# HGRN scores of a token with itself and with its pair's other token: column sums of products in place of matrix products

## What is computed

```
q, f_f, f_b, v, g = split(h @ w_in)          # 16 heads of 128 features
q = silu(q)
f = lb + (1 - lb) * sigmoid(f_raw);  k = 1 - f        # once for each direction
S_t = diag(f_t) S_{t-1} + k_t v_t^T,   o_t = S_t^T q_t   # forwards and backwards, summed
```

## Time and profile before

| | us |
|---|---|
| median of 3 runs | 2587.51 (2587.24 to 2588.46) |
| the profiled execution, whole | 2589.72 |
| its span, first to last instruction | 2587.9 |
| TensorE matmuls busy in it | 2551.4 |
| VectorE busy | 1684.3 |
| ScalarE busy | 1231.3 |

### The profile page before, as it was taken

One profiled execution on the slowest core, in us unless ns is written; L12 is line 12 of the kernel. 1 busy time (PEld: TensorE's weight loads), 2 busy tenths in 40 slices (PEclk: granted clock), 3 DMA queues, 4 the chain that ended last, 5 costly groups with the idle time before them and its releaser, 6 DMA issues. The chain is left out here.

```text
span 2587.9 us, 32843 instructions
## 1 busy us (share of the span) xinstructions
PE 2551.4 (99%) x13382; PEld 2169.6 (84%) x13382; DVE 1684.3 (65%) x1807; ACT 1231.3 (48%) x1446; POOL 27.8 (1%) x25
## 2 busy tenths in 40 slices
PE   7999999999999999999999999999999999999997
PEld 6878888888888888888888888888788888888886
DVE  6645766555555555555777778785676777777776
ACT  7545344443443444444445454544555444444443
POOL 0000000000000000000000000000000000000000
PEclk9999999999999999999999999999999999999999
DMA  9535445556555555555545454545465555655553
GB/s 358 170 132 163 161 151 177 187 183 194 191 189 191 187 192 189 187 190 176 171 150 175 140 182 134 178 164 180 140 210 188 186 187 188 193 188 187 185 190 114
DMA packets 127413, 465.63 MB, mean 180 GB/s; under 512 B 14208, under 2 KB 14464, under 8 KB 126368
## 3 DMA queue, kind: packets, MB, share of 16 engines
q1 hardware_dynamic: 127264, 463.54, 54.8%
HBM read 461.38 MB, written 2.10 MB: 179 GB/s over the span
## 5 line engine op out<-in xcount | busy, mean ns | idle before, releaser
L1246 DVE TENSOR_TENSOR w_low<-raw,w_high 128x1024 fp32r<-128x1024 f32 x856 | 1042.3, 1224 | 729.2 <-ACT w_high L973 727.1
L973 ACT ACTIVATE w_high<-raw 128x1024 fp32r<-128x1024 f32 x856 | 904.4, 1058 | 922.0 <-PE job L714 507.3
L717 PE MATMUL job<-actA,w_high 128*128 128x512 f32 x3328 | 1180.7, 399 | 1.1 <-DVE actA L1306 1.1
L720 PE MATMUL job<-actA,w_low 128*128 128x256 f32 x3328 | 934.7, 281 | 0.0
L717 PEld LDWEIGHTS job<-actA,w_high 128*128 128x128 f32 x3328 | 626.3, 188 | 156.1 <-DVE actA L1306 1.4
L720 PEld LDWEIGHTS job<-actA,w_low 128*128 128x128 f32 x3328 | 629.5, 189 | 0.7
L712 PE MATMUL job<-w_high,actB 128*128 128x512 f32 x1184 | 463.3, 391 | 10.1 <-DVE w_low L1246 9.9
L713 PE MATMUL job<-w_low,actB 128*128 128x512 f32 x1184 | 461.7, 390 | 0.0
L714 PE MATMUL job<-w_high,actB 128*128 128x512 f32 x1184 | 461.6, 390 | 0.0
L712 PEld LDWEIGHTS job<-w_high,actB 128*128 128x128 f32 x1184 | 222.8, 188 | 57.0 <-issue 9.9
L714 PEld LDWEIGHTS job<-w_high,actB 128*128 128x128 f32 x1184 | 222.8, 188 | 46.9
(11 more groups left out here) (193 smaller groups left out, 1232.0 us busy)
## 6 DMA issues: line engine op xcount, KB each, us to landing
raw<-in_weights SPq DMA_DIRECT2D x856, 512.0 KB, 3.4
M<-in_mem_t SPq DMA_DIRECT2D x4, 512.0 KB, 7.3
slots<-in_mem SPq DMA_DIRECT2D x2, 1024.0 KB, 14.3
M<-in_x_t SPq DMA_DIRECT2D x4, 512.0 KB, 13.8
H<-in_x SPq DMA_DIRECT2D x1, 2048.0 KB, 15.1
out<-H SPq DMA_DIRECT2D x4, 512.0 KB, 2.9
slots<-in_w_small SPq DMA_DIRECT2D x1, 1024.0 KB, 14.1
slots<-in_post_mix_g SPq DMA_DIRECT2D x1, 1024.0 KB, 4.7
```

The lines of the kernel that those rows point to most:

```text
L717: nc.tensor.matmul(J[job.buf][:, x, :], w_high[:, slot, cols], act_both[job.act][:, c, :, :].rearrange("p a t -> p (a t)"), start=begins, ...
L720: mm = nc.tensor.matmul(J[job.buf][:, x, T:2 * T], w_low[:, slot, cols], act_high[job.act][:, c, :], start=False, stop=ends, skip_group_ch ...
L973: nc.scalar.activation(w_high[:, s % AHEAD, :], raw[:, s % RAW_SLOTS, :], ACT.Copy)\
L1246: nc.vector.tensor_tensor(w_low[:, s % AHEAD, :], raw[:, s % RAW_SLOTS, :], w_high[:, s % AHEAD, :].bitcast(F32), ALU.subtract).then_inc(l ...
```

## The change

The two scores that need no matrix product are formed as column sums. For the score of a token with itself VectorE multiplies kk and q elementwise (`sum_product`, "self"); for the other token of the pair it multiplies the queries by the copied keys, read in pairs in reversed order ("pair"). The sum over the 128 features, which lie on partitions, is a product with a 128 x 128 matrix of ones: every row of the result holds all column sums, and the diagonal copy and the mask of level 0 pick from it as before. To be multiplied in the kind of operands that the windows use, each product is split by ScalarE (high) and VectorE (low) into chunks 12 to 15 of the B activations, which are free in these steps (`sum_split`). `column_sums` is then 4 matmuls of 512 columns: high and low for each half of the heads. It takes the place of 8 matmuls in `hgrn_diagonal` and of 8 in `hgrn_level` 0; the matrix of ones becomes an `F32R` tile, written by ScalarE at the start in place of GpSimd. Levels 1 to 6 are as before.

In the plan sum_product(self) comes late in step 25, its split early in 26, the diagonal stays late in 26, sum_product(pair) comes late in 26, its split early in 28. Level 0 and all levels behind it move one window later (28, 30, ..., 40), and so do across (42), attend (44), gate (46) and turn (49).

```diff
     "q_make": dict(hgrn_ready=1),
+    "sum_product": dict(sum_made=1),
+    "sum_split": dict(sum_high=1, sum_low=1),
...
         p.put_early(j.end + 1, "q_make")
+        p.put(base + 25, "sum_product", "self")
+        p.put(base + 25, "hgrn_keys", 0)
+        p.put_early(base + 26, "sum_split", "self")
         p.put(base + 26, "hgrn_diagonal")
+        p.put(base + 26, "sum_product", "pair")
+        p.put_early(base + 28, "sum_split", "pair")
         for level in range(LEVELS):
-            p.put(base + 25 + 2 * level, "hgrn_keys", level)
-            p.put(base + 27 + 2 * level, "hgrn_level", level)
+            if level > 0:
+                p.put(base + 26 + 2 * level, "hgrn_keys", level)
+            p.put(base + 28 + 2 * level, "hgrn_level", level)
...
-        p.put(base + 41, "hgrn_across")
+        p.put(base + 42, "hgrn_across")
...
-        ones = sb("ones", [P, P])
+        ones_r = sb("ones", [P, P], F32R)
+        ones = ones_r[:, :].bitcast(F32)
...
+        summed = {"self": m_slot(3), "pair": a_slot(4)}
+        sum_high, sum_low = (x["B"][:, 12:16, :] for x in (act_high, act_low))
...
-            pool.memset(ones[:, :], 1.0).then_inc(ones_set, 1)
...
                 wait(pe, n, "rows_ready", 0)
-                for h in range(HEADS4):
-                    for t in range(TT):
-                        at = (2 * h + t) * P
-                        tok = slice(h * T + t * P, h * T + (t + 1) * P)
-                        mm = nc.tensor.matmul(att[:, at // COLS, at % COLS:at % COLS + P], hg["kk"][:, tok],
-                                              hg["q"][:, tok], start=True, stop=True)
+                wait(pe, n, "sum_low", 0)
+                column_sums(0)
+
+            def column_sums(bank):
+                pe.wait_ge(ones_set, 1)
+                for half_ in range(2):
+                    heads = slice(2 * half_, 2 * half_ + 2)
+                    nc.tensor.matmul(att[:, bank + half_, :], ones_r[:, :], sum_high[:, heads, :],
+                                     start=True, stop=False)
+                    mm = nc.tensor.matmul(att[:, bank + half_, :], ones_r[:, :], sum_low[:, heads, :],
+                                          start=False, stop=True)
                 mm.then_inc(S["scored"], 1)
...
                 wait(pe, n, "o_low", 0)
+                if level == 0:
+                    wait(pe, n, "sum_low", 0)
+                    column_sums(bank)
+                    return
...
+                elif name == "sum_split":
+                    wait(act, n, "sum_made", 0)
+                    wait(act, n, "scored", 0)
+                    nc.scalar.activation(sum_high, by_feature(summed[a[0]]), ACT.Copy).then_inc(S["sum_high"], 1)
...
+            nc.scalar.activation(ones_r[:, :], half[:, 0:1].to_broadcast([P, P]), ACT.Copy, scale=-2.0)\
+                .then_inc(ones_set, 1)
...
+                elif name == "sum_product":
+                    product = summed[a[0]]
+                    wait(dve, n, "kk_made", 0)
+                    wait(dve, n, "hgrn_ready", 0)
+                    wait(dve, n, "o_turned", 0)
+                    wait(dve, n, "attended", 0)
+                    if a[0] == "self":
+                        ins = nc.vector.tensor_tensor(product, hg["kk"], hg["q"], ALU.mult)
+                    else:
+
+                        wait(dve, n, "keys_set", 0)
+                        by_pair = lambda ap: ap.rearrange("p (n two m) -> p n two m", two=2, m=1)
+                        keys = hg["sq"]
+                        keys = bass.AP(keys.tensor, keys.offset + 1, [list(keys.ap[0]), [2, 512], [-1, 2], [1, 1]])
+                        ins = nc.vector.tensor_tensor(by_pair(product), crossed(0, 0, 1024, 1), keys, ALU.mult)
+                    ins.then_inc(S["sum_made"], 1)
+                elif name == "sum_split":
+                    wait(dve, n, "sum_high")
+                    nc.vector.tensor_tensor(sum_low, by_feature(summed[a[0]]), sum_high.bitcast(F32),
+                                            ALU.subtract).then_inc(S["sum_low"], 1)
```

More of the change, by code:

```diff
@@ L310, in plan_hgrn @@
         j = p.job("tokens", "A", "hgrn_w_in", 4 * D + g * COLS)
-        p.put(base + 41, "hgrn_across")
+        p.put(base + 42, "hgrn_across")
         p.put_early(j.end, "silu_gate", j.buf, "g")
-        p.put(base + 43, "hgrn_attend")
-        p.put(base + 43, "o_square", "hgrn")
-        p.put(base + 43, "o_norm", "hgrn")
-        p.put(base + 45, "o_gate", "hgrn")
-        p.put(base + 48, "o_turn", "hgrn", g)
+        p.put(base + 44, "hgrn_attend")
+        p.put(base + 44, "o_square", "hgrn")
+        p.put(base + 44, "o_norm", "hgrn")
+        p.put(base + 46, "o_gate", "hgrn")
+        p.put(base + 49, "o_turn", "hgrn", g)
 def plan_hgrn_out(p):
@@ L756, in rows @@
                     wait(pe, n, kind, 0)
-                nc.tensor.matmul(att[:, 1, 0:T], ones[:, :], diag[:, :, :].rearrange("p t c -> p (t c)"),
+                nc.tensor.matmul(att[:, 1, 0:T], ones, diag[:, :, :].rearrange("p t c -> p (t c)"),
                                  start=True, stop=True).then_inc(S["rows_done"], 1)
@@ L1028, in stage @@
                     wait(act, n, "attended", 0)
+                    wait(act, n, "sum_low", 0)
                     wait(act, n, "rstd_h" if who == "h" else "rstd_in", 0)
```

## The result

| | before | changed |
|---|---|---|
| median, us | 2587.66 (2587.24 to 2588.46) | 2611.3 (2609.75 to 2612.14, 4 runs) |
| ratio to before | | 1.0093, 95% interval 1.0081 to 1.0105 |
| span of the profiled execution, us | 2587.9 | 2610.3 |

The changed kernel is 24 us slower, 6 us for each group of heads; the forecast was 2609.5 us. (Of the experiments, e1 and e7 have a profiled execution in which TensorE ran slow from start to end, so no duration is taken from their traces.)

The account below looks back on a forecast made before the run. TensorE, busy 99%, was taken to bound the kernel. Per group +5.33 first wait, +1.9 clock, +1.13 second wait, -2.84 savings gave +5.5 us, four groups +22.0, so 2609.5 us on the 2587.51 median; range 2601 to 2616.

Parts of the forecast that it names:

- the walk's rule: Step w on ScalarE and VectorE starts with window w+5's split, which waits until TensorE has done window w.
- The savings: TensorE, diagonal, level 0 and the wait before the product across: 0.88 + 1.76 + 0.2 = 2.84 us saved a group.
- The first wait: Before the diagonal's column sums, TensorE waits for product self, its rounding and low part: 5.33 us a group, at least 3.5.
- The clock: Behind the first wait TensorE's clock falls to 0.50, costing 1.9 us a group, range 1.4 to 2.3.
- Rival (1): The waits come, but TensorE's clock holds or recovers at once: 3.6 us a group, 2602.0 us; chance 0.09.
- The second wait: Before level 0's column sums, TensorE waits 1.13 us a group for the pair's low part.
- The pair product: VectorE's product reading queries in pairs across two slots takes 1.2 to 2.2 us and is no part of the second wait.
- Margins of the levels: VectorE starts level 0 0.44 us behind the block, before 0.19; tightest key margin, level 2, falls from 1.42 to 1.17; no wait.
- The sum: All terms together: +5.5 us a group (4.7 to 6.1), +22.0 us for four groups, median 2609.5 us.
- None of this is on the path by its mass: Added VectorE and ScalarE work costs nothing by amount: VectorE has a 3.0 us gap, TensorE's weights are windows ahead; order counts.
- rival (2): Sums are ready when TensorE comes after window 26, so only savings of 2.84 us a group remain: 2576.1 us; chance 0.06.
- rival (3): Levels start to wait too, VectorE entering level 0 over 1.17 us later than forecast: 2613 to 2617 us; chance 0.08.

Follow-up runs that it names:

- e1: Changed kernel, but column sums read the A activations without waiting for the low parts (wrong scores), added VectorE and ScalarE work kept: 2585.02 us, ratio 0.9997.
- e7: Same kernel as e1 (changed kernel, column sums on the A activations without waits for the low parts), run again: 2588.26 us, ratio 1.0006.
- e9: Changed kernel, all arithmetic kept, product self made inside q_make, its split and VectorE's level 0 issued earlier, diagonal and levels a window later: 2573.22 us, ratio 0.9952.
- e6: Changed kernel with the product self computed twice, one behind the other, to lengthen the first wait: 2613.03 us, ratio 1.0107.
- e4: Changed kernel with product self and its split one step earlier in the plan, to shorten the first wait: 2599.39 us, ratio 1.0049.
- e10: Same kernel as e1 (changed kernel, column sums on the A activations without waits for the low parts), run again for a trace: 2587.31 us, ratio 1.0007.

## Why the prediction was right, and where it wasn't

- **What bounds the kernel, and the walk's rule** (step w runs behind window w on the feeding engines). Held: moving steps by one or two, with the product's arithmetic unchanged, took the same kernel from 2611 to 2573 us.
- **The savings, 2.84 us a group.** Held: 2.91 by e9's distance between groups, 12.4 us for 11.4 by its median.
- **The first wait, 5.33.** 5.44 start to start. The backlog behind q_make was real: the product began at 1278.09, 1.62 us after TensorE had stopped.
- **The clock, 1.9** as the middle of 1.4 and 2.3, which took the loss to grow with the length of the wait. It was 2.19, 2.56, 2.78 and 2.87 us in the four groups, outside these bounds in three of them, 10.4 us in all for 7.6. This is the term that was sized lowest, and its reason doesn't hold: the same wait of 5.44 us gave four different losses, and the wait of 6.7 us in e6 only 1.8. The rule of the Trainium skill (TensorE: Matmul & The Clock Gate, HAM oscillation — how this bites in real kernels), that a pause between bursts costs half of the throttled time, agrees: 4.4 us at 0.50, 2.19 lost, and 5.9 us at 0.50, 2.87 lost. Rival (1), a clock that holds, falls: it fell behind each of the four (the first column sum takes 0.76 us in each group), and in e4 even after 3.2 us of idleness.
- **The second wait, 1.13.** 1.24, and 1.08 in the bracket.
- **The pair product, between 1.2 and 2.2 us.** 1.46, with no say in the time of this kernel.
- **Margins of the levels.** VectorE began level 0 0.24 us behind the block where 0.44 was put down; no wait, as said.
- **The sum.** By the measured terms the four groups cost 6.03 + 6.40 + 6.62 + 6.71 = 25.8 us, where 22.0 was predicted: 2.8 too little for the clock, 0.9 for the waits. (The bounds of 4.7 and 6.1 us a group are wider than the terms given for them: 1.4 and 2.3 for the clock make 5.0 and 5.9.) That the median lies only 1.8 us above the forecast, and the span grew by 22.4, is in part luck, from places for which the forecast had no term. 0.9 us lie ahead of group 0 (TensorE comes at 1276.47, before at 1277.34). 2.2 us lie behind the groups: from the end of the wait of 3.8 us in the turn to the FFN (L736, changed L747) to the last instruction the kernel before takes 2587.9 - 1825.28 = 762.6 us, the changed one 2610.3 - 1849.88 = 760.4. There the clock was low for less long behind the same wait of 3.8 us, and behind the next one, of 1.9 us, it fell in the kernel before and not in the changed one. Before and changed, some four microseconds behind the end of the first wait, then behind the second:

```profile
1829.00:1833.00 4.00, 3.74 (x18) 3.30 (x19) 4.00 (x10) 2.26 (x6) 0.00 (x0) 0.80 0.00 0
...
1850.72:1854.51 3.79, 3.79 (x12) 3.20 (x13) 1.03 (x1) 0.38 (x1) 0.00 (x0) 0.55 0.78 223
```

```profile
1853.88:1858.00 4.12, 4.12 (x27) 3.75 (x28) 4.03 (x10) 2.50 (x8) 0.00 (x0) 1.00 0.02 4
...
1874.64:1880.00 5.36, 5.36 (x30) 4.65 (x31) 1.70 (x2) 1.45 (x2) 0.00 (x0) 1.00 0.52 169
```

- **What was wrong without showing in the number.** "None of this is on the path by its mass", with VectorE's gap of 3.0 us as the reason, and from it rival (2), 2576.1 us if no wait came. The 4.9 us of added VectorE work are hidden *because* TensorE waits ahead of them. With the wait gone, and the steps where the change put them, the same work comes back as a wait of 2.6 us at level 1, and the time is 2587 us (e10), not 2576. It was rival (3)'s mechanism under rival (2)'s condition; I had held the two apart. The margin of VectorE was to be read against TensorE's earlier arrival, too.

## What to carry to other kernels

When a step is taken from the bounding engine and given to one with idle time, cost two things apart: the chain of handovers until the first result, in the order in which the program has it, and how late the helper then is for its *next* deadline, with the wait and without it. An engine that is idle only because it waits for the bounding one has no time to give where its work is due at once; the same arithmetic in other steps made a kernel that is 0.5% faster out of one that is 0.9% slower. A stall of a few microseconds of TensorE is to be priced with the clock: here 1.7 to 2.9 us on top of waits of 3.3 to 6.7 us, and the longest didn't cost the most.

## What the runs showed of the hardware that was not expected

The length of the wait didn't set what the clock cost. Behind waits of 5.44 us, the same in each group, it cost 2.19 to 2.87 us; behind waits of 6.7 us (e6) 1.8; behind waits of 3.3 us (e4) 1.7. What differs is where in the wait the clock fell: 2.4 us before its end in group 0 of the changed kernel, 0.9 in group 3, 3.2 in group 0 of e6. The clock need not fall during the idle time at all: in e4 it fell 0.7 us after TensorE had resumed and stayed low for some 3.4 us of full work. After the 1.1 us before level 0 it didn't fall; after the 2.6 us before level 1 in e10 it fell in one group of four; after the 1.9 us in the turn to the FFN it fell in the kernel before and not in the changed one. All this is read from one profiled execution of each kernel; what decides when the clock falls was not tried.
